# Unrolling the mixer of a decoder layer, with unnormalised k and q and the product of state and q behind the triangular solve

## Chip, cores, metric

The kernel runs on one core of a Trainium2 chip. The metric is the device time of one launch in microseconds. All arithmetic is float32; large matrix products are made from three products of rounded parts, as told below.

## What is computed

One layer (D = 1024) for a prompt of 1024 tokens and 8 short sequences of 4 tokens each (the "samples", 32 tokens, each with a cached state). Cut from the reference:

```python
h = rmsnorm(x, norm_mix)
proj = h @ w_in                       # columns: q, k, v | a, b | z | sc_b, sc_c, sc_h, all but a, b 512 wide
qkv = silu(causal_dwconv(qkv_in, w_conv_qkv))            # width 4
q = l2norm(q) * 128 ** -0.5;  k = l2norm(k)              # x / sqrt(sum x^2 + EPS), per head of 128
log_a = -exp(a_log) * softplus(proj_a + dt_bias);  beta = sigmoid(proj_b)
# gated delta rule, 4 heads, in chunks; g is the running sum of log_a in the chunk, decay = exp(g_i - g_j):
#   A = I + strict(beta * kk * decay); u, w = A^-1 applied to beta*v and beta*exp(g)*k
#   v_new = u - w S;  o = (q exp(g)) S + (q k^T decay) v_new;  S = S exp(g_last) + (k exp(g_last - g))^T v_new
o = rmsnorm(o, w_gdn_norm) * silu(z)
y_sc = sc_b * causal_dwconv(sc_c * sc_h, w_conv_sc)      # width 3
x = x + concat([o, y_sc]) @ w_out
x = x + relu(rmsnorm(x) @ w_up) ** 2 @ w_down
x = x + sigmoid(rmsnorm(x) @ w_ple_gate) * (p @ w_ple_proj)
```

## The kernel before

Each engine has a program of its own, written by hand, and the programs meet at semaphores; the order in each program is the order of execution.

**Units.** The projections run in units of 128 output columns. A unit is three thirds of 352 tokens, each 24 products on PE (TensorE): 8 blocks of k times three products of rounded parts (high by high, low part of the activations by high, high by low part of the weights), 72 products in all. For each unit SP (SyncE, whose queue issues the loads in order) loads `w_raw`, ACT (ScalarE) rounds it to `w_hi` (all its operations have the helper's line, L972), DVE (VectorE) makes `w_lo` (L1335), and each third is taken out of PSUM by DVE (for q, k and v: L1393). A unit of q, k or v is then convolved by DVE (its last three operations are L1416) and passed through a Silu by ACT. Two units are in flight: the buffers `w_raw`, `w_hi`, `w_lo`, `pre`, `cv` are doubled.

**Stages.** (1) Norm of the input: tiles of x are squared by ACT (`x_sqr`), turned, scaled and split into `act_hi`, `act_lo`; a small product makes the gates a and b. (2) Twelve units of q, k, v in that order (the products are at L555). (3) A loop of four passes. A pass has the products of four units (z, c, h, b), 288 of them at L663, dealt out by the table `STEPS` and `FILL` between the steps of two chunks of 128 tokens, so that PE has products while other engines work on the chunks. (4) The sample tokens' delta rule (L763 to L860), with the first unit of the output projection in its gaps. (5) The rest of the output projection, the MLP, and the input embedding.

**A chunk in a pass.** Three products with a matrix of ones (L682, L683, L685) sum the squares of q and k over a head's 128 rows and spread g along a row; DVE and ACT normalise k and q with them (`kn`, L1530 on DVE); PE makes k k^T and q k^T (L689, L690). DVE makes the decay matrix and from it `PT` (L1534) and `AT` (L1536). The inverse of the triangular matrix is built in six doublings, the levels (`X` and its transpose `XT`; POOL, that is GpSimd, starts them at L1935 and L1937 and masks each level's factor at L1918; PE has the products y at L703 and z at L712 and L715; DVE copies y and adds z at L1549). Then the state steps: two transposes (L724, L725), k by the state S (L726), the solve (L732), q by S and the score by v_new in one group (L741, L742), the update of S (L745), a ones sum for the output's norm (L749). The PE program of a pass, shortened:

```python
with pe.Fori(0, NSC) as j:
    fill("begin0")
    for x in range(2):
        ...
        mm(bk[0][:, :], ones[:, :], Tb[0][:, :, :], start=True, stop=True)          # L682
        ...
        fill(f"prep_norm{x}")
        pe.wait_ge(sm.qk_made, 2 * c1)
        per_head(lambda h, s: mm(bk[0][:, s], kn[x][:, h, :], kn[x][:, h, :], start=True, stop=True))
    for l in range(1, LEVELS):
        for x in range(2):
            pe.wait_ge(sm.lt_made, n1)
            per_head(lambda h, s: mm(bk[x][:, s], Tb[2 + x][:, h, :], X[x][:, h, :], ...)).then_inc(sm.y_mm, 1)
            fill(f"y{x}_{l}")
```

z goes from `cv` to DRAM (`z_spill`) and comes back chunk by chunk.

## Time and profile before

| | us |
|---|---|
| median of 3 runs | 1646.56 (1646.44 to 1648.52) |
| the profiled execution, its own time | 1649.36 |
| its span (first to last instruction) | 1647.8 |
| PE busy in it | 1568.8 (95%) |
| DVE, ACT, POOL busy | 726.5, 484.8, 299.2 |
| PE's granted clock over the span | 9 tenths or more in all but a few of 40 slices; 5 and 7 tenths in slices 15 and 16 |

The time before the first instruction and after the last is the 1.6 us between 1649.36 and 1647.8. In the trace a stretch begins and ends at instructions: the second unit's last third leaves PSUM at 62.70 us, the passes run to 572.3 us, the sample tokens and the first output unit to 652.9 us, where the second output unit starts; what comes behind it (994.9 us) the change doesn't touch. Durations of pipelined products overlap, so the distance between products, not the duration of one, is what a product takes.

### The profile page before, as it was taken

The page shows a single profiled execution, that of the slowest core. Times are in us where ns is not written, and L with a number is a line of the kernel's source. Part 1 is how long each engine was busy: PE and PEld are TensorE (multiplying, and loading weights), DVE is VectorE, ACT ScalarE, POOL GpSimd, SP SyncE. Part 2 cuts the span into 40 slices and gives each one's busy share as a digit, 9 for nine tenths or more (in the row PEclk, how much of TensorE's full clock was granted, in tenths as well). Part 3 has the DMA queues.
Part 4 walks back from the last instruction along what each step waited for, and adds up shares of the span by engine and source line. Part 5 has one row for each costly group of instructions (what it writes and reads, how often), then busy time and mean ns, then how long its engine had stood idle before and what let it go on. Part 6 is the DMA issues. An engine that isn't in the chain of part 4 may idle for free.

```text
span 1647.8 us, 26980 instructions
## 1 busy us (share of the span) xinstructions
PE 1568.8 (95%) x9857; PEld 1518.2 (92%) x9857; DVE 726.5 (44%) x1201; ACT 484.8 (29%) x818; POOL 299.2 (18%) x361
## 2 busy tenths in 40 slices
PE   7899899999999858999999999999999999999997
PEld 6899889899999846998999999999999999998997
DVE  5566555454555534225333333333333433335435
ACT  6223322223232241226321303122121313126435
POOL 5100062534526233221000000000000000032213
PEclk9999999999999957999999999999999999999998
DMA  6111110201013033321111111111111111111102
GB/s 165 38 49 40 37 39 14 64 13 52 13 39 105 0 109 93 95 76 39 52 39 51 39 51 49 42 52 39 52 44 47 47 43 52 39 51 55 49 26 106
DMA packets 135718, 86.65 MB, mean 53 GB/s; under 512 B 16507, under 2 KB 130843, under 8 KB 135654
## 3 DMA queue, kind: packets, MB, share of 16 engines
q1 hardware_dynamic: 134502, 81.48, 17.3%
q0 software_dynamic: 1152, 4.33, 0.7%
q8 instruction: 39, 0.64, 0.2%
q14 instruction: 25, 0.20, 0.0%
HBM read 74.58 MB, written 11.21 MB: 52 GB/s over the span
## 4 chain that ended last, share of the span: by engine, by line
PE 85%; DVE 6%; ACT 3%; issue 3%; POOL 1%; DMA 1%; SPq 1%; DVEq 0%; ACTq 0%; POOLq 0%
PE pg L555 64%; PE pg L663 8%; PE bk L703 3%; PE bk L712 2%; DVE act_lo L1656 1%; PE bk L870 1%; PE bk L715 1%; ACT act_hi L972 1%; DVE cv L1416 1%; ACT w_hi L972 1%; POOL XT L1937 1%; DVE qkv L1610 1%; PE bk L682 1%; PE bk L683 0%; DVE w_lo L1335 0%
## 5 line engine op out<-in xcount | busy, mean ns | idle before, releaser
L555 PE MATMUL pg<-act_hi,w_hi 128*128 128x352 f32 x1464 | 480.9, 328 | 17.9 <-issue 4.9
L555 PE MATMUL pg<-act_lo,w_hi 128*128 128x352 f32 x1464 | 473.8, 324 | 0.0
L555 PE MATMUL pg<-act_hi,w_lo 128*128 128x352 f32 x1440 | 464.3, 322 | 0.0
L555 PEld LDWEIGHTS pg<-act_hi,w_hi 128*128 128x128 f32 x1464 | 278.8, 190 | 22.4 <-issue 6.5
L555 PEld LDWEIGHTS pg<-act_lo,w_hi 128*128 128x128 f32 x1464 | 279.1, 191 | 0.0
L555 PEld LDWEIGHTS pg<-act_hi,w_lo 128*128 128x128 f32 x1440 | 272.5, 189 | 0.0
L555 PE MATMUL pg<-u_hi,w_hi 128*128 128x352 f32 x768 | 249.3, 325 | 0.0
L555 PE MATMUL pg<-u_hi,w_lo 128*128 128x352 f32 x768 | 248.9, 324 | 0.0
L555 PE MATMUL pg<-u_lo,w_hi 128*128 128x352 f32 x768 | 247.8, 323 | 0.0
L1991 POOL TENSOR_TENSOR ssq<-ssq,sq 128x352 f32<-128x352 f32 x72 | 77.8, 1094 | 890.2 <-ACT sq L972 889.3
L972 ACT ACTIVATE w_hi<-w_raw 128x1024 fp32r<-128x1024 f32 x111 | 116.7, 1051 | 323.7 <-PE pg L555 301.5
L1703 DVE TENSOR_TENSOR xres<-xres,pg 128x352 f32 (+1 forms) x192 | 99.2, 520 | 200.9 <-PE pg L555 200.9
L1335 DVE TENSOR_TENSOR w_lo<-w_raw,w_hi 128x1024 fp32r<-128x1024 f32 x110 | 141.9, 1290 | 81.3 <-ACT w_hi L972 81.3
L555 PEld LDWEIGHTS pg<-u_hi,w_hi 128*128 128x128 f32 x768 | 145.0, 189 | 0.0
L555 PEld LDWEIGHTS pg<-u_lo,w_hi 128*128 128x128 f32 x768 | 144.5, 188 | 0.0
L555 PEld LDWEIGHTS pg<-u_hi,w_lo 128*128 128x128 f32 x768 | 143.9, 187 | 0.0
L663 PE MATMUL pg<-act_hi,w_lo 128*128 128x352 f32 x384 | 131.0, 341 | 0.0
L663 PE MATMUL pg<-act_lo,w_hi 128*128 128x352 f32 x384 | 130.3, 339 | 0.0
L663 PE MATMUL pg<-act_hi,w_hi 128*128 128x352 f32 x384 | 129.3, 337 | 0.0
L972 ACT ACTIVATE sq<-tm 128x352 f32<-128x352 f32 x96 | 47.8, 498 | 231.5 <-DVE tm L1689 231.5
L1693 DVE TENSOR_TENSOR u_lo<-sq,u_hi 128x352 f32 x96 | 50.4, 525 | 129.6 <-ACT u_hi L972 129.6
L972 ACT ACTIVATE Tb<-bk 128x512 f32<-128x512 f32 (+2 forms) x76 | 44.2, 583 | 182.0 <-PE bk L703 111.8
(295 smaller groups left out, 1845.8 us busy)
## 6 DMA issues: line engine op xcount, KB each, us to landing
w_raw<-in_w_up SPq DMA_DIRECT2D x32, 512.0 KB, 4.0
w_raw<-in_w_down SPq DMA_DIRECT2D x32, 512.0 KB, 3.4
w_raw<-in_w_in SPq DMA_DIRECT2D x29, 512.0 KB, 3.9
x_tok<-in_x_prompt SPq DMA_DIRECT2D x8, 512.0 KB, 7.8
w_raw<-in_w_out SPq DMA_DIRECT2D x8, 512.0 KB, 4.9
x_col<-in_x_prompt SPq DMA_DIRECT2D x8, 512.0 KB, 3.7
w_raw<-in_w_ple_gate SPq DMA_DIRECT2D x8, 512.0 KB, 4.0
out<-y_tok SPq DMA_DIRECT2D x8, 512.0 KB, 2.9
```

The lines of the kernel that those rows point to most:

```text
L555: last = mm(pg[bank][:, 0:TH], w, a, start=i == 0, stop=i == len(terms) - 1)
L663: last = mm(pg[n][:, 0:TH], w, (act_hi, act_lo, act_hi)[r][:, k, cols(n)], start=k == 0 and r == 0, stop=k == KD - 1 and r == 2)
L682: mm(bk[0][:, :], ones[:, :], Tb[0][:, :, :], start=True, stop=True)
L703: per_head(lambda h, s: mm(bk[x][:, s], Tb[2 + x][:, h, :], X[x][:, h, :], start=True, stop=True)).then_inc(sm.y_mm, 1)
L712: last = per_head(lambda h, s: mm(zb[:, s], XT[x][:, h, :], Tb[x][:, h, :], start=True, stop=True))
L715: last = per_head(lambda h, s: mm(ztb[:, s], Tb[x][:, h, :], XT[x][:, h, :], start=True, stop=True))
L870: last = turn(bk[n][:, c:c + e - a], x_col[x][a:e, t, :], ident[a:e, a:e])
L972: return nc.scalar.activation(out, in_, func, **kw)
L1335: tt(w_lo[b % 2][:, :, :], w_raw[b % 2][:, :, :], w_hi[b % 2][:, :, :].bitcast(f32), SUB) \
L1693: tt(rows(u_lo[c % 2][:, k, cols(n)]), sq[g % 2][:, :], rows(u_hi[c % 2][:, k, cols(n)]).bitcast(f32), SUB).then_inc(sm.u_lo_made, 1)
L1703: tt(x_t, x_t, pg[g % 3][:, 0:TH], ADD).then_inc(sm.evacuated, 2)
L1991: tt(ssq[:, cols(n)], ssq[:, cols(n)], sq[g % 2][:, :], ADD).then_inc(sm.ssq_added, 1)
```

## The change

The mixer's loops are unrolled, and a table built in Python (`PLAN`) says which steps stand between which products, across chunks and units:

- Order of units: q and k first (8 units), then the four of v, then the four of z, then c, h, b in turn (12).
- The 288 products of the v units are dealt out around the inverse of chunks 0 and 1; those of the z units around the whole of the samples' delta rule (before: behind the passes); then three slots of 236 products with the inverse of the next two chunks and the state steps of the two before; the last slot has 108 products and the state steps of chunks 6 and 7. The first output unit follows (48 products of the last b unit stand in the piece called mix).
- k and q stay unnormalised. The sum of k's squares is taken by DVE from the diagonal of k k^T (`ssk`, a by-product of an operation it makes anyway), its reciprocal goes into beta; q's norm goes into the output's norm (`comb`). The two ones sums for them are gone. The rows of g come from DRAM: SP writes `g_dram` once and loads each chunk's rows, spread over all partitions (`LY`, `E`), so the third ones sum is gone too.
- The product of state and q stands right behind the triangular solve, in a PSUM bank of its own, and the score's product is added later.
- v of a chunk is turned by PE (`vturn`) ahead of its state steps; z goes through the Silu before it is spilled.
- At the start: ACT's squares of x tiles 4 to 8 stand behind the splits of `act_hi`, and the first 24 products of the first unit stand ahead of the last product of the gates; the gates' chain of logs and exponentials is spread over units 1 to 4.

The diff, cut to its core:

```diff
-STEPS = (["begin0", "prep_norm0", "prep_kk0", "prep_norm1", "prep_kk1", "prep_x0", "prep_x1"]
-         + [f"{w}{x}_{l}" for l in range(1, LEVELS) for w, x in (("y", 0), ("y", 1), ("z", 0), ("z", 1))]
-         + [f"{s}{x}" for x in range(2) for s in ("s_in", "s_solve", "s_out", "s_norm")])
-BODY_MM = 4 * KD * 9
-FILL = {"begin0": 50, "prep_norm0": 38, "prep_norm1": 38, "prep_kk0": 16, "prep_kk1": 21, "prep_x0": 4, "prep_x1": 2,
-        "s_in0": 13, "s_in1": 22, "s_solve0": 8, "s_solve1": 8, "s_out0": 8, "s_out1": 8, "s_norm0": 2}
-for _s in STEPS:
...
+def inverse_steps(s):
+    c = (2 * s, 2 * s + 1)
+    steps = [("prep", c[0], 0), ("prep", c[1], 0), ("turned", c[0], 0), ("turned", c[1], 0)]
+    for l in range(1, LEVELS):
+        steps += [("y", c[0], l), ("y", c[1], l), ("z", c[0], l), ("z", c[1], l)]
+    return steps
+def state_steps(s):
+    steps = []
+    for c in (2 * s, 2 * s + 1):
+        steps += [(k, c, 0) for k in ("into", "kturn", "solve", "update", "sum", "norm", "scale")]
+    return steps
...
+    slot([(("begin", 0, 0), 64)] + [(st, {"prep": 14, "turned": 2}.get(st[0], 8)) for st in inverse_steps(0)],
+         9 * KD * NSC)
+    smp = [("s_norm", 16), ("s_conv", 4), ("s_kk", 20), ("s_conv", 4), ("s_xt", 14), ("s_conv", 4), ("s_y", 12),
+           ("s_z", 12), ("s_state", 12), ("s_turn", 10), ("s_solve", 12), ("s_out", 20), ("s_onorm", 14)]
...
+    slot([(("s_wait", 0, 0), 6 * KD), (("s_begin", 0, 0), 4)] + steps, 9 * KD * NSC)
+    for s in range(1, NPAIR):
+        steps = [(("vturn", 2 * s - 2, 0), 6), (("vturn", 2 * s - 1, 0), 6)]
+        inv, rec = inverse_steps(s), state_steps(s - 1)
+        steps += [(rec.pop(0), 4), (rec.pop(0), 6)]
+        for i, st in enumerate(inv):
+            steps.append((st, {"prep": 14, "turned": 2}.get(st[0], 6)))
+            if i % 2 == 1 and rec:
+                steps.append((rec.pop(0), 3))
+        assert not rec
+        slot(steps, SLOT_FILL)
+    steps = [(("vturn", NTT - 2, 0), 2), (("vturn", NTT - 1, 0), 2)]
+    steps += [(st, {"scale": 0}.get(st[0], 8)) for st in state_steps(NPAIR - 1)]
+    last = 9 * KD * 3 * NSC - (NPAIR - 1) * SLOT_FILL
+    slot(steps + [(("tail", 0, 0), 0)], last - 6 * KD)
+    order.extend([(("mix", 0, 0), 3 * KD), (("mix", 1, 0), 3 * KD), (("mix", 2, 0), 0)])
+    out, at = [], 0
+    for (k, c, l), n in order:
+        out.append((k, c, l, at, at + n))
+        at += n
...
+                if k == "begin":
+                    sp.wait_ge(sm.rows_step, 2)
+                    sp.dma_start(g_dram[:, :], LY[1][0:NTT * H, 0, :]).then_inc(sm.rows_out, 16)
+                    sp.wait_ge(sm.rows_out, 16)
+                    load_rows(0)
+                    load_rows(1)
+                    load_in(U_V + 1)
+                    load_in(U_V + 2)
...
+                elif k == "vturn" and c == 0:
+                    for h in range(H):
+                        sp.wait_ge(sm.s_out_made, 2 * (h + 1))
+                        sp.dma_start(os_s[0, :, h, :, :].rearrange("b d e -> d b e"), S_in[:, h, :, :]) \
+                            .then_inc(sm.sample_states_out, 16)
+                    for x in range(2):
+                        sp.wait_ge(z_spilled[x], 16 * (NSC // 2))
+                    sp.dma_start(qkv[:, H:2 * H, TP:T], z_dram[:, :, TP:T].rearrange("h p t -> p h t")) \
+                        .then_inc(sm.zs_loaded, 16)
+                    sp.wait_ge(sm.q_o, 1)
+                    load_rows(2)
+                    load_rows(3)
+                    sp.wait_ge(sm.sample_states_out, 16 * H)
+                    sp.dma_start(E[:, :, :], g_dram[None, 0:H, :].to_broadcast([P, H, P])).then_inc(sm.ge_in, 16)
+                elif k == "solve" and c < NTT - 1:
...
-                fill("begin0")
-                for x in range(2):
-                    c1 = 2 * j + x + 1
-                    pe.wait_ge(sm.squared, 2 * c1)
-                    if x == 0:
-                        pe.wait_ge(sm.o_made, 2 * j + 1)
-                    else:
-                        pe.wait_ge(sm.at_made, 2 * j + 1)
-                    mm(bk[0][:, :], ones[:, :], Tb[0][:, :, :], start=True, stop=True)
-                    mm(bk[1][:, :], ones[:, :], Tb[1][:, :, :], start=True, stop=True)
-                    pe.wait_ge(sm.diag_made, c1)
-                    mm(bk[2][:, :], ones[:, :], X[x][:, :, :], start=True, stop=True) \
-                        .then_inc(sm.norms_summed, 1)
-                    fill(f"prep_norm{x}")
-                    pe.wait_ge(sm.qk_made, 2 * c1)
-                    per_head(lambda h, s: mm(bk[0][:, s], kn[x][:, h, :], kn[x][:, h, :], start=True, stop=True))
...
+                        pe.wait_ge(sm.x_updated, upd(c - 2, LEVELS - 1))
+                    per_head(lambda h, v: mm(A[x][:, v], qkv[:, H + h, chunk(c)], qkv[:, H + h, chunk(c)],
+                                             start=True, stop=True)).then_inc(sm.kk_mm, 1)
+                    if c > 0:
+                        pe.wait_ge(sm.pt_made, c)
+                    if c > 1:
+                        pe.wait_ge(sm.x_updated, upd(c // 2 * 2 - 1, SQUARE))
+                    per_head(lambda h, v: mm(A[2][:, v], qkv[:, H + h, chunk(c)], qkv[:, h, chunk(c)],
+                                             start=True, stop=True)).then_inc(sm.kq_mm, 1)
...
+                elif k == "solve":
+                    pe.wait_ge(sm.r_vec, 4 * (c + 1))
+                    pe.wait_ge(sm.x_updated, upd(c, LEVELS - 1))
+                    per_head(lambda h, v: mm(R[1][:, v], XT[s][x][:, h, :], rv[:, h, :], start=True, stop=True)) \
+                        .then_inc(sm.solve_mm, 1)
+                    pe.wait_ge(sm.qg_made, c + 1)
+                    pe.wait_ge(sm.ktok_made, 4 * (c + 1))
+                    per_head(lambda h, v: mm(R[0][:, v], S[:, h, :], qkv[:, h, chunk(c)], start=h == 0, stop=False)) \
+                        .then_inc(sm.os_mm, 1)
+                elif k == "update":
+                    pe.wait_ge(sm.w_made, c + 1)
+                    per_head(lambda h, v: mm(R[1][:, v], ktok[:, h, :], wn[:, h, :], start=True, stop=True)) \
+                        .then_inc(sm.upd_mm, 1)
+                elif k == "sum":
+                    per_head(lambda h, v: mm(R[0][:, v], wn[:, h, :], PT[s][x][:, h, :], start=False, stop=h == H - 1)) \
+                        .then_inc(sm.op_mm, 1)
+                elif k == "norm":
+                    pe.wait_ge(sm.comb_made, c + 1)
+                    pe.wait_ge(sm.osq_made, c + 1)
...
+            def before_sum(c):
+                if c == 0:
+                    act.wait_ge(sm.sample_states_out, 16 * H)
+                else:
+                    act.wait_ge(sm.onorm_mm, c)
+                op(comb[:, :, :], qkv[:, 0:H, chunk(c)], ACT.Square, scale=float(P) * EPS ** 0.5) \
+                    .then_inc(sm.qsq_made, 1)
+                act.wait_ge(sm.ge_in, 16 * (c + 1))
+                op(E[:, :, :], E[:, :, :], ACT.Exp).then_inc(sm.e_made, 1)
...
+                    if name == "v" and n == 1 and i > 0:
+                        silu_unit(b - 1)
+                        log_exp()
+                    if name == "z" and i == 0 and n == 1:
+                        silu_unit(b - 1)
+                    if name == "z" and n == 2:
+                        act.wait_ge(sm.evacuated, 12 * b + 12)
+                        op(cv[i % 2][:, 0:T], cv[i % 2][:, 0:T], ACT.Silu).then_inc(sm.z_silu, 1)
+                        log_exp()
...
+                if name == "v":
+                    qkv_third(b, n)
+                    if n == 2:
+                        unit_done(b, 0)
+                        convolve(b)
+                    return
...
+                if k == "prep":
+                    dve.wait_ge(gb_in[x], 16 * (c // 2 + 1))
+                    dve.wait_ge(sm.causal_made, 1)
+                    if c >= 2:
+                        dve.wait_ge(sm.lt_made, lev(c - 2, LEVELS - 1))
+                    for h in range(H):
+                        stt(AT[x][:, h, :], LY[x][:, h, :], g_tok[:, c, h:h + 1], m_inc[:, :], SUB, MIN) \
+                            .then_inc(sm.diff_made, 1)
+                    dve.wait_ge(sm.kk_mm, c + 1)
+                    if c >= 2:
+                        dve.wait_ge(sm.y_mm, lev(c - 2, LEVELS - 1))
+                    for h in range(H):
+                        stt(X[x][:, h, :], A[x][:, h * P:(h + 1) * P], 1.0, ident[:, :], MUL, MUL,
+                            accum_out=ssk[:, c, h:h + 1]).then_inc(sm.diag_made, 1)
+                    dve.wait_ge(sm.diag_made, 4 * (c + 1))
+                    ts_(sbk[:, c, :], ssk[:, c, :], EPS, None, ADD).then_inc(sm.k_step, 1)
+                    dve.wait_ge(sm.k_step, 3 * c + 1)
+                    nc.vector.reciprocal(sbk[:, c, :], sbk[:, c, :]).then_inc(sm.k_step, 1)
+                    dve.wait_ge(sm.k_step, 3 * c + 2)
+                    tt(sbk[:, c, :], sbk[:, c, :], beta[:, c, :], MUL).then_inc(sm.k_step, 1)
+                    dve.wait_ge(sm.kq_mm, c + 1)
+                    dve.wait_ge(sm.decay_made, c + 1)
+                    if c >= 4:
+                        dve.wait_ge(sm.op_mm, c - 3)
+                    tt(PT[s][x][:, :, :], heads(A[2]), AT[x][:, :, :], MUL).then_inc(sm.pt_made, 1)
```

On DVE, in the loop of before: behind the normalising of a chunk's k (L1530), with one third of a fill unit taken out (L1481) and one weight split:

```order
L1530 TENSOR_TENSOR kn<-qkv,Tb 128x512
L1343 REGISTER_ALU
L1481 TENSOR_TENSOR cv<-pg,r_b 128x352 [waits mm_done]
L1329 ISA
L1335 TENSOR_TENSOR w_lo<-w_raw,w_hi 128x1024 [waits w_hi_made]
L1534 TENSOR_TENSOR PT<-bk,Tb 128x512 [waits masked,kk_made]
```

The same engine after the change, in the first slot (v units), from the preparation of chunk 0 (`PT00`, `AT0`) to that of chunk 1 (`AT1`, `X1`):

```order
L1762 TENSOR_TENSOR PT00<-bk2,AT0 128x512 [waits decay_made,kq_mm]
L1766 SCALAR_TENSOR_TENSOR AT0<-bk0,sbk,AT0 128x128 [waits pt_made,k_step]
L1766 SCALAR_TENSOR_TENSOR AT0<-bk0,sbk,AT0 128x128 x3
L1590 TENSOR_TENSOR pre0<-pg2,r_b 128x320 [waits mm_done]
L1592 TENSOR_TENSOR pre0<-pg2,r_b 128x8x4
L1533 TENSOR_TENSOR w_lo1<-w_raw1,w_hi1 128x1024 [waits w_hi_made]
L1609 TENSOR_SCALAR cv0<-pre0,cq_w 128x1080 [waits silu_made,evacuated]
L1612 SCALAR_TENSOR_TENSOR cv0<-pre0,cq_w,cv0 128x1080 [waits conv_step] x3
L1744 SCALAR_TENSOR_TENSOR AT1<-LY1,g_tok,m_inc 128x128 [waits causal_made,gb_in1]
L1744 SCALAR_TENSOR_TENSOR AT1<-LY1,g_tok,m_inc 128x128 x3
L1750 SCALAR_TENSOR_TENSOR X1,ssk<-bk1,ident 128x128 [waits kk_mm]
L1750 SCALAR_TENSOR_TENSOR X1,ssk<-bk1,ident 128x128 x3
```

In the loop of before no convolution stood between the parts of a pass; now the whole of one (L1609, L1612) stands between the preparation of chunk 0 and that of chunk 1.

On SP's queue before, at the head of the passes, the weights' loads follow each other:

```order
L442 UNCONDITIONAL_BRANCH
L442 ISA
L414 ISA [waits w_lo_made]
L414 DMA w_raw<-in_w_in 128x8x128
```

After the change, at the head of the first slot (first fence) and of the third, the first with state steps (second fence), with the writes of the samples' states (`out<-S_in`), the samples' z (`qkv<-z_spill`) and the rows of g (`LY`, `E`) in the same queue:

```order
L585 DMA g_rows<-LY 32x128 [waits rows_step]
L566 DMA LY<-g_rows 128x512 [waits rows_out]
L566 DMA LY<-g_rows 128x512
L524 DMA w_raw<-in_w_in 128x8x128 [waits w_lo_made] x4
```

```order
L612 DMA qkv<-z_spill 128x4x32 [waits z_spilled1,z_spilled0]
L566 DMA LY<-g_rows 128x512 [waits q_o]
L566 DMA LY<-g_rows 128x512
L618 DMA E<-g_rows 128x512 [waits sample_states_out]
L628 DMA qkv<-z_spill 128x4x128 [waits kt_mm]
L621 DMA E<-g_rows 128x512 [waits qg_made]
L524 DMA w_raw<-in_w_in 128x8x128 [waits w_lo_made]
```

Loads of weights now stand behind transfers that wait for other engines: the first behind the way of g's rows to DRAM and back, the later ones behind the spilled z and the states.

## Rows read from the trace of the kernel before

**Rows 1.** The page: busy time of the engines.
```profile
PE 1568.8 (95%) x9857; PEld 1518.2 (92%) x9857; DVE 726.5 (44%) x1201; ACT 484.8 (29%) x818; POOL 299.2 (18%) x361
```

**Rows 2.** Busy time in stretches; the first line names the columns.
```profile
core 0: us, PE busy (x) PEld busy (x) DVE busy (x) ACT busy (x) POOL busy (x), PEclk, DMA share, GB/s
0.00:62.70 62.70, 50.61 (x297) 47.35 (x298) 31.41 (x48) 30.02 (x53) 23.76 (x80) 0.95 0.52 124
62.70:213.00 150.30, 140.96 (x854) 136.75 (x853) 95.19 (x142) 48.92 (x64) 17.48 (x39) 0.97 0.16 43
308.90:404.50 95.60, 92.97 (x642) 88.02 (x641) 48.24 (x90) 26.19 (x42) 39.86 (x39) 0.98 0.11 33
572.30:652.90 80.60, 51.92 (x248) 41.37 (x248) 35.89 (x48) 24.28 (x40) 27.73 (x21) 0.65 0.33 93
```

**Rows 3.** The waits of PE: total us, times, longest.
```profile
PE bk L703 <- POOL Tb L1918: 7.4, 4, 1.9
...
PE pg L555 <- DVE pre L1393: 4.4, 1, 4.4
```

**Rows 4.** The chain that ended last: start, length, what.
```profile
24.66 1.14 ACT x_sqr L972 x2
...
40.75 0.86 PE bk L626 x2
...
803.69 689.64 PE pg L555 x4296
```

**Rows 5.** PE in order of time, full clock: a level's products, transposes.
```profile
425.14 1.05 PE L703 MATMUL bk<-X,Tb 128*128 128x128 f32 x8
...
426.36 1.05 PE L703 MATMUL bk<-X,Tb 128*128 128x128 f32 x8
...
464.31 0.60 PE L725 MATMUL bk<-ident,X 128*128 128x128 f32 x4
464.74 1.06 PE L726 MATMUL bk<-S,kn 128*128 128x128 f32 x8
```

**Rows 6.** PE in order of time, 17 products behind a wait of 8.2 us.
```profile
616.22 0.49 PE L555 MATMUL pg<-act_lo,w_hi 128*128 128x352 f32 x1
616.51 0.49 PE L555 MATMUL pg<-act_hi,w_lo 128*128 128x352 f32 x1
...
620.62 0.42 PE L555 MATMUL pg<-act_lo,w_hi 128*128 128x352 f32 x1
```

**Rows 7.** DVE in order of time, the end of one unit.
```profile
62.70 0.49 DVE L1393 TENSOR_TENSOR pre<-pg,r_b 128x320 f32<-128x320 f32 x1 [3.22 <-PE pg L555]
...
63.80 1.22 DVE L1335 TENSOR_TENSOR w_lo<-w_raw,w_hi 128x1024 fp32r<-128x1024 f32 x1 [0.50 <-ACT w_hi L972]
...
65.75 4.10 DVE L1416 SCALAR_TENSOR_TENSOR cv<-pre,cq_w,cv 128x1080 f32<-128x1080 f32 x3
```

**Rows 8.** DVE in order of time, operations of a chunk.
```profile
406.41 1.12 DVE L1522 TENSOR_SCALAR Tb<-bk,g_tok 128x128 f32<-128x128 f32 x4 [5.12 <-ACT Tb L972]
...
423.82 0.69 DVE L1549 TENSOR_TENSOR X<-X,bk 128x512 f32<-128x512 f32 x1 [5.35 <-PE bk L712]
```

**Rows 9.** POOL in order of time, the start of one inverse.
```profile
413.80 1.29 POOL L1935 TENSOR_TENSOR XT<-AT,m_lev 128x512 f32<-128x512 f32 x1 [1.12 <-DVE AT L1536]
415.17 2.14 POOL L1937 TENSOR_TENSOR XT<-ident,XT 128x512 f32<-128x512 f32 x1
417.27 2.48 POOL L1918 TENSOR_TENSOR Tb<-AT,m_lev 128x512 f32<-128x512 f32 x2
```

**Rows 10.** ACT in order of time: a table load, the next operation.
```profile
604.67 1.28 ACT L1146 ACT_TABLE_LOAD   x1
605.97 1.06 ACT L972 ACTIVATE act_hi<-qkv 128x1024 fp32r<-128x1024 f32 x1
```

**Rows 11.** DMA issues: KB each, median us to landing.
```profile
w_raw<-in_w_in SPq DMA_DIRECT2D x29, 512.0 KB, 3.9
...
z_spill<-cv POOLq DMA_DIRECT2D x4, 528.0 KB, 4.0
```

1759 lines of the change are left out of this document (940 added, 819 removed).

## The prediction

> **What bounds the kernel now.** The table of busy times comes first: PE has products during 95% of the span, no other engine more than 44% [rows 1]. So the time is PE's work plus its waits, and the change can win only by taking work off PE, or by filling the stretches in which it stands. The busy times in stretches show where these are [rows 2]. In a pass (308.90 to 404.50, 95.60 us) PE is busy for 92.97 at a clock of 0.98, with next to no slack. In the samples' stretch (572.30 to 652.90, 80.60 us) it is busy for 51.92, and at a clock of 0.65. Up to 62.70 it is busy for 50.61. The list of PE's waits [rows 3] names what a pass still waits for, POOL's masked factor (7.4 us in 4 waits), and one wait of 4.4 us at the evacuation of a q unit. In the chain of waits the products of the MLP follow at 689.64 / 4296 = 0.1605 us each [rows 4], the price of a product below.
>
> **Prices of PE's work.** Two level products in order of time stand 426.36 - 425.14 = 1.22 us apart [rows 5]; two fill products (0.32) are between, so a group of four heads costs 0.90. The transposes of four heads cost 464.74 - 464.31 = 0.43 [rows 5]. A sum with the matrix of ones over 512 columns is one product in the code and two records in the trace; the chain gives 0.86 for the two [rows 4], nearly a group's 0.90, which has as many columns, so a sum costs 0.86 and not half of it.
>
> **The work removed.** Before, a chunk has 20 groups of four heads (k k^T, q k^T, six y, seven z, k S, solve, two in the output, update), two sets of transposes and four ones sums: 20 x 0.90 + 2 x 0.43 + 4 x 0.86 = 22.3 us. A pass is then 288 x 0.1605 + 2 x 22.3 = 90.8, against 95.6 measured: 4.8 lost. After, the groups and transposes are as many, and one ones sum is left: 19.7. Eight chunks save 8 x 3 x 0.86 = 20.6 us. A reciprocal and an accumulated sum on DVE replace them: its four diagonal operations are like L1522, 1.12 us [rows 8], and lie under 14 products (2.2 us) in a steady slot.
>
> **The front.** The squares of five x tiles (1.14 us for two pieces in the chain, [rows 4]) leave ACT's path ahead of the splits: 5 x 1.14 = 5.7 us, and 24 products of the first unit (3.9) go into the wait for the last split. Sum 9.7; low bound 3.8, if the tiles' loads are what is late next. So what is at 62.70 comes at 53.0.
>
> **The account from 62.7 to 652.9.** It is 590.2 us. Products: 27 units x 72 x 0.1605 = 312.0. Chunks: 8 x 22.3 = 178.6. The samples' own PE work and the turns of x: the stretch's 51.92 less 72 products (11.6) is 40.3 at the slow clock and, times 0.65, 51.92 gives 33.7, less 11.6 is 22.1. I take 32, between them. Sum 522.6, so 67.6 us are lost today to waits and the slow clock, about 35 of them in the samples' stretch, 4 x 4.8 = 19 in the passes. After, the work is 312.0 + 157.6 + 32, and 1 for the turn of g into rows, 502.6, and 53.0 + 502.6 = 555.6. With L for the losses after, the second output unit starts at 555.6 + L, against 652.9. **The whole question is L: at 97.3 the gain is gone.**
>
> **What L is made of.** The samples move behind 288 products, so their chain of small steps (a wait of 8.2 us among them today) has cover: slot 1 has 288 x 0.1605 = 46 us of it for some 13 steps, and only what waits longer than the 12 to 20 products between steps is lost. Against this stand new waits, and each of them is made by one engine's bulk work standing ahead of a chain step:
>
> - Slot 0, 27 us. (a) SP sends g's rows to DRAM and back before the next weights. A load of weights lands in 3.9 us, a spill in 4.0 [rows 11]; the way there and back ahead of them makes the weights of unit 10 some 7 us late, and with them `w_hi`, `w_lo` (1.22, [rows 7]), and the last k unit's convolution: PE waits 5 to 7. (b) In the order of DVE the convolution (from a third's evacuation at 62.70 to its last operations' end at 65.75 + 4.10 = 69.85 is 7.15 us, [rows 7]) stands between the preparations of chunks 0 and 1, and POOL's start of the inverse (1.29 + 2.14, then 2.48 for two masks, [rows 9]) behind that: the first y of chunk 1 waits about 7. (c) Two more convolutions stand ahead of the step that puts a z product into X (0.69, [rows 8]): 7.15 + 0.7 less a cover of 4.2 to 4.4 is 3.7, twice. Each such wait is followed by products at about half clock (1.2 GHz, not 2.4): in the stretch behind the wait of 8.2 us they stand 616.51 - 616.22 = 0.29 apart up to 620.62 [rows 6], 15 to 17 of them, so 17 x 0.13 = 2 us more. Sum 6 + 2 + 7 + 2 + 2 x (3.7 + 1.3) = 27.
> - Slot 1, 7 us: the samples' squares wait for the last v unit (its last third, 24 products or 3.9 us, and 7.15 to the end of the convolution are 11.05 with the Silu behind it; 52 products ahead of the samples' sums cover 8.3), then Silus of z with table loads (1.28 each, [rows 10]).
> - Slot 2, 14 us: `E` and the rows of chunks 2 and 3 stand in SP's queue behind the last z unit's spill: evacuation 0.5, `w_hi` 1.05, table 1.28 [rows 10], Silu 1, spill 4.0 [rows 11] make 7.8, two loads of rows at 2 to 4 each put `E` at about 12.9. PE is through its covered steps in about 6 and waits in pieces of 2 to 3.
> - Slots 3 and 4: today's 4.8 for a pass, 5 each. Last slot: 8 products (1.3 us) cover each step of a chain whose steps take 1.5 to 2.5: 8.
>
> L = 27 + 7 + 14 + 10 + 8 = 66. Then 555.6 + 66 = 621.6, 31.3 earlier than 652.9; what follows is untouched. 1649.4 - 31.3 = 1618.1 for the profiled execution, whose own time is 2.8 above the median of the runs shown, so **1615.3**.
>
> **A rule against it.** ACT changes its table more often: 18 loads between the v units and the end of slot 1. In the trace a load takes 1.28 us and the next operation starts 0.02 us behind its end (604.67 + 1.28 = 605.95, start 605.97) [rows 10], so 23 us of ACT's time in 92 us, beside some 30 of other work: hidden, but for the places above. The Trainium skill (ScalarE: Activation LUTs, "What ACT_TABLE_LOAD costs") puts a drain of the pipeline on top of the load, about twice the load alone; the row shows none of it behind a load. By the page it would be about 1.38 us more for each, 25 us over all if every one lay on PE's path, and the time about 1640.
>
> **The rivals.**
>
> A. The forecast, L from 50 to 80: 1600 to 1630.
>
> B. The new waits are covered: the row loads take under 2 us and the squares wait for nothing. Then L is about today's share of the passes (19) and half of slot 0, some 35: 1616 - 31 = 1584. For it: before, a pass loses only 4.8 with the same chain. Against: DVE's order really has whole convolutions between steps.
>
> C. The loads of rows are late at every slot, not at slots 0 and 2 alone, or the samples' chain is longer than its 46 us: 20 more, 1630 to 1643. For it: the samples' stretch takes 80.6 us today, less 11.6 of products, for 46 us of cover, though it also holds 28 us of waits and runs at 0.65. The table loads at the page's price would end here too.
>
> D, on the other side: slower. DVE's and ACT's bulk work isn't covered in any slot. There are 20 unit ends from slot 0 on; the split of weights and evacuation (2.3 us each) in front of a chain step would give 46, four convolutions before and in slot 0 with their Silus and the z Silus 34, and 20 waits with slow products behind each 2.3 x 20 = 46: L = 126, which is 29 over 97.3, so 1675.6. It decides from L = 97.3, an average wait of about 1.2 us at each of the roughly 80 steps. Against it: steps have 6 to 14 products, 1 to 2.2 us, besides the other chunk's group. A pass today has the same kind of bulk work at L = 4.8.
>
> E. The change gives nothing: L within 94 and 101 (0.2%, 3.3 us, is about what a measurement of this kernel tells from no change).
>
> **How the numbers follow.** A 0.50, B 0.25, C 0.17, D 0.05, E 0.03. Faster is A + B + C = 0.92, same 0.03, slower 0.05. The range leaves out about 1 in 10 below (B's lower half) and 1 in 10 above: 1585 to 1641. The unknowns reach as far: the front at 3.8 adds 6; the parts of L at slot 0 and slot 2, the largest, are each good to some 10; the samples' work at 22 or 40 moves little, since it stands on both sides.
>
> **What the profile after would show.** The end of the first unit near 41.5 us and of the second near 53; if the second stays above 57, the loads bound the front. One ones sum for a chunk in place of four, and no others. PE's waits in slot 0 for ACT's Silu (about 5), at a y product for DVE's `X` (about 7) and twice at a y or z for DVE's step on X (3.7); in slot 1 one for ACT before the samples' ones sums; at the start of slot 2 for `E` or `comb`. The second output unit at about 621 in place of 652.9, and behind it 995 us as now. The prediction is wrong if L is spread evenly over the slots (C or D), or if the clock stays low behind short waits, so that a wait costs more than its 2 us, or if the first slot's waits are missing (B). In slots 3 and 4 a distance above 85 us (236 products and two chunks are 77.3) would speak for D.

## The result and the profile after

The changed kernel takes 1623.52 us (median of 4 runs, 1622.55 to 1624.63) against 1646.82 (4 runs, 1646.44 to 1648.52): ratio 0.9857, 95% interval 0.9840 to 0.9874, 23.3 us faster. The forecast was 1615.3 with a range of 1585 to 1641: the right side and case (A), 8.2 us too low. The profiled execution took 1623.29 us, its span 1621.5.

The page after, first the busy times (before: [rows 1]):

```profile
PE 1548.1 (95%) x9812; PEld 1508.4 (93%) x9812; DVE 730.2 (45%) x1261; ACT 489.4 (30%) x872; POOL 291.6 (18%) x346
```

PE's share is the same 95%, with 20.7 us less of busy time. The stretches, which answer to [rows 2]: first the rest of the k and q units, then the slot of the v units, the slot of the z units and the samples, and the first slot with state steps:

```profile
core 0: us, PE busy (x) PEld busy (x) DVE busy (x) ACT busy (x) POOL busy (x), PEclk, DMA share, GB/s
60.60:130.30 69.70, 69.70 (x443) 69.58 (x442) 48.04 (x71) 16.89 (x27) 3.49 (x19) 1.00 0.13 33
130.30:236.20 105.90, 81.87 (x530) 80.55 (x529) 59.32 (x101) 27.41 (x38) 25.89 (x27) 0.87 0.21 54
236.20:316.80 80.60, 77.92 (x449) 67.19 (x448) 31.21 (x54) 25.96 (x35) 13.58 (x18) 0.92 0.25 75
316.80:407.00 90.20, 81.43 (x578) 79.04 (x577) 48.19 (x103) 29.16 (x55) 39.62 (x38) 0.96 0.18 52
```

PE stands for 24.0 us in the v slot and hardly at all in the samples' slot (2.7 us; before, 28.7 in their stretch). The waits of PE, over the whole execution (compare [rows 3]):

```profile
PE bk L852 <- DVE XT L1778: 11.6, 2, 6.3
PE bk L852 <- DVE X L1770: 9.5, 2, 8.6
PE bk L902 <- DVE wn L1791: 8.4, 3, 3.7
...
PE bk L910 <- POOL comb L2180: 3.7, 3, 2.1
PE bk L838 <- ACT qkv L1136: 3.6, 1, 3.6
...
PE bk L885 <- POOL S L2189: 2.2, 1, 2.2
```

Before, the chain of waits had the MLP's 4296 products start at 803.69 [rows 4]; after:

```profile
777.09 689.62 PE pg L688 x4296
```

They start 26.6 us earlier and take as long as before. The table follows the prediction's landmarks: its value, and where the changed kernel's trace has it. L is a stretch's length less its work, priced as in the prediction.

| landmark or loss | forecast | measured |
|---|---|---|
| second unit's last third leaves PSUM | 53.0 | 60.55 |
| v slot: L | 27 | 105.9 - 73.2 = 32.7 |
| slot 2: L | 14 | 90.2 - 77.3 = 12.9 |
| slots 3, 4: L | 10 | (81.0 - 77.3) + (82.9 - 77.3) = 9.3 |
| last slot: L | 8 | 41.3 - 25.0 - 12.5 = 3.8 |
| z slot and first output unit: L, the rest | 7 | 7.0 |
| second output unit starts | 621.6 | 628.9 |

The sum of L is 628.9 - 60.6 - 502.6 = 65.7, forecast 66. The miss of the total is in the first line; the lines for L miss in both directions and cancel.

### The profile page after: what moved, and what is told of

The parts are those of the page before. It is cut to its first block, busy times and chain, and to the rows that moved or that the text cites. A ratio compares the mean times of both kernels' runs of the same rounds, so it can differ in the third digit from the quotient of the medians.

```text
span 1621.5 us, 25803 instructions
## 1 busy us (share of the span) xinstructions
PE 1548.1 (95%) x9812; PEld 1508.4 (93%) x9812; DVE 730.2 (45%) x1261; ACT 489.4 (30%) x872; POOL 291.6 (18%) x346
## 3 DMA queue, kind: packets, MB, share of 16 engines
q1 hardware_dynamic: 139254, 85.15, 18.3%
## 4 chain that ended last, share of the span: by engine, by line
PE 84%; DVE 7%; ACT 2%; issue 2%; POOL 2%; DMA 0%; SPq 0%; DVEq 0%; POOLq 0%; ACTq 0%
PE pg L688 62%; PE pg L806 10%; PE bk L852 3%; PE bk L866 2%; DVE cv L1612 1%; DVE act_lo L1881 1%; PE bk L870 1%; PE bk L1013 1%; DVE AT L1744 1%; POOL act_lo L2186 1%; PE bk L824 1%; PE bk L1117 1%; PE bk L993 1%; ACT w_hi L1136 0%; PE bk L902 0%
## 5 line engine op out<-in xcount | busy, mean ns | idle before, releaser
L688 PE MATMUL pg<-act_hi,w_hi 128*128 128x352 f32 x1344 | 438.6, 326 | 10.4 <-issue 4.6
L688 PE MATMUL pg<-act_lo,w_hi 128*128 128x352 f32 x1344 | 432.6, 322 | 0.0
L688 PE MATMUL pg<-act_hi,w_lo 128*128 128x352 f32 x1320 | 423.8, 321 | 0.0
L688 PEld LDWEIGHTS pg<-act_hi,w_hi 128*128 128x128 f32 x1344 | 253.4, 189 | 14.4 <-issue 8.5
L688 PEld LDWEIGHTS pg<-act_lo,w_hi 128*128 128x128 f32 x1344 | 254.0, 189 | 0.0
L688 PEld LDWEIGHTS pg<-act_hi,w_lo 128*128 128x128 f32 x1320 | 248.0, 188 | 0.0
L806 PE MATMUL pg<-act_hi,w_hi 128*128 128x352 f32 x480 | 164.9, 344 | 0.0
L806 PE MATMUL pg<-act_hi,w_lo 128*128 128x352 f32 x480 | 164.6, 343 | 0.0
L806 PE MATMUL pg<-act_lo,w_hi 128*128 128x352 f32 x480 | 164.4, 342 | 0.0
L806 PEld LDWEIGHTS pg<-act_lo,w_hi 128*128 128x128 f32 x480 | 94.1, 196 | 3.6 <-issue 3.4
```

What stands on the lines that cost most here:

```text
L688: last = mm(pg[bank][:, 0:TH], w, a, start=i == 0, stop=i == len(terms) - 1)
L806: last = mm(pg[n][:, 0:TH], w, (act_hi, act_lo, act_hi)[r][:, k, cols(n)], start=k == 0 and r == 0, stop=k == KD - 1 and r == 2)
```

## Experiments

All are the changed kernel with one edit, or a few where said, timed beside the kernel before. Its medians beside them were 1647.92, 1648.46 and 1646.56 us, so a difference of 1 to 2 us between two kernels' medians says little, and the intervals of the first five edits below overlap the base's. Their effects are read from "landmarks", the times of the same instructions in two profiled executions. These scatter too: in eight executions with the same start the first ones sums begin at 41.84 to 43.07 us, the v slot takes 105.6 to 107.7 us where no edit touches it, and the z slot takes 80.6 us in some executions and 76.8 in others (see the last section).

**The changed kernel again**, as a base. 

> The changed kernel itself, unaltered, as the base for the kernels that are run beside it. Its median should lie within 1.5 us of 1623.5; every difference below is taken against this one.

Measured: 1624.04 (1622.42 to 1626.72), ratio 0.9861 (0.9842 to 0.9881). The ones sums at the start begin at 42.56 us, the turns of x ahead of the second output unit at 628.43.

**The squares back in their loop.**

```diff
-                if t < 4:
-                    square(t)
+                square(t)
...
-            for t in range(4, NTT + 1):
-                square(t)
```

> The changed kernel with the squares of x tiles 4 to 8 back in ACT's loop, between the splits of act_hi. By the prediction's term (five squares of 1.14 us leave ACT's path) it is 5 to 6 us slower than the changed kernel. The rival, read from the trace after: the splits waited for DVE and for PE's turns, not for ACT (ACT idles 3.8 and 1.9 us between splits), and the postponed squares now hold up the norm of x (r_tok at 38.7 us, before 33.3), on which the ones sums at 42.0 wait. By the rival it is the same within 1.5 us, or faster.

Measured: 1622.54 (1619.26 to 1626.60), ratio 0.9856 (0.9836 to 0.9876). The ones sums start at 41.12, 1.4 us earlier than the base and 0.7 earlier than the earliest of the eight executions. Two later kernels with the same start have them at 41.30 and 42.67, so whether anything is gained isn't clear; the prediction's 5.7 us slower isn't there for this edit alone.

**The first group back.**

```diff
-            first_group(0)
             pe.wait_ge(sm.xlo_even, NTT + 1)
             pe.wait_ge(sm.xlo_odd, NTT + 1)
             ab_group(2)
+            first_group(0)
             first_group(1)
```

> The changed kernel with the first 24 products of the first unit back behind the last product of the gates a and b. By the prediction's term they filled a wait of 3.5 us, so it is 3 to 4 us slower. The rival: PE's start of the ones sums at 42.0 us is set by ACT's postponed squares, and PE only waits in another place; then within 1 us of the changed kernel.

Measured: 1626.05 (1624.12 to 1627.42), ratio 0.9869 (0.9851 to 0.9887). The ones sums start at 44.59, 2.0 us later than the base and 1.5 later than the latest of the eight executions, about half of the term of 3.9. It lies between the two expectations.

**Both edits of the start undone.** 

> The changed kernel with both of its edits to the start undone: ACT's squares in their loop, and the first 24 products behind the gates' last. If the two are independent: the group costs 2.0, the squares give 1.4 back, so the ones sums start 0.6 us later than in the changed kernel, at 42.6 to 43.2 us. By the prediction's account 9.7 us later. The rival: with the group back PE's order is what bounds and the squares are hidden either way, about 44.5.

Measured: 1628.25 (1626.04 to 1628.91), ratio 0.9883 (0.9863 to 0.9903). The ones sums start at 47.95, 5.4 us later than the base. All three expectations fall: the two edits stand in for each other. With the group early, PE works while ACT squares; with the squares late, the split is ready early. Either covers most: PE waits for the last split of the activations 1.6 us with the group alone back, not at all with the squares alone back, and 3.6 us with both back, and it then goes on at half clock. The second unit's last third leaves PSUM at 66.18, so with both edits undone the start is 3.5 us slower than that of the kernel before (62.70).

**The ones sums back.**

```diff
+                    for _ in range(3):
+                        mm(A[x][:, :], ones[:, :], qkv[:, H:2 * H, chunk(c)], start=True, stop=True)
                     per_head(lambda h, v: mm(A[x][:, v], qkv[:, H + h, chunk(c)], qkv[:, H + h, chunk(c)],
```

> The changed kernel with three sums with the matrix of ones over 512 columns added to each chunk's preparation (24 in all, results overwritten, nothing else altered), which prices the ones sums that the change removed. By the account (PE is what bounds, 0.86 us each) 24 x 0.86 = 20.6 us slower. The rival: a part of them would lie in PE's waits (the preparations of chunks 0 to 3 are followed by waits), then 13 to 17 us.

Measured: 1626.95 (1624.30 to 1627.81), ratio 0.9872 (0.9853 to 0.9891): 2.9 us, below both expectations. Each set of three does take 2.6 us where it stands (412.60 to 415.18 in its trace). By landmarks the v slot grows by 5.7 us (of which up to 2 can be scatter), slot 2 shrinks by 1.4, slots 3 and 4 grow by 3.9 and 1.4: 9.6 of 20.6. The wait for v_new shrinks from 8.4 us in three to 1.7 in two, since DVE is done while PE sums. The z slot is 3.9 us shorter in this execution, and that isn't the sums' doing (see the clock, below).

**The product of state and q one step later.**

```diff
                     per_head(lambda h, v: mm(R[1][:, v], XT[s][x][:, h, :], rv[:, h, :], start=True, stop=True)) \
                         .then_inc(sm.solve_mm, 1)
-                    pe.wait_ge(sm.qg_made, c + 1)
-                    pe.wait_ge(sm.ktok_made, 4 * (c + 1))
-                    per_head(lambda h, v: mm(R[0][:, v], S[:, h, :], qkv[:, h, chunk(c)], start=h == 0, stop=False)) \
-                        .then_inc(sm.os_mm, 1)
                 elif k == "update":
                     pe.wait_ge(sm.w_made, c + 1)
+                    pe.wait_ge(sm.ktok_made, 4 * (c + 1))
                     per_head(lambda h, v: mm(R[1][:, v], ktok[:, h, :], wn[:, h, :], start=True, stop=True)) \
                         .then_inc(sm.upd_mm, 1)
+                    pe.wait_ge(sm.qg_made, c + 1)
+                    per_head(lambda h, v: mm(R[0][:, v], S[:, h, :], qkv[:, h, chunk(c)], start=h == 0, stop=False)) \
+                        .then_inc(sm.os_mm, 1)
```

> The changed kernel with the product of state and q moved from behind the triangular solve to behind the product that updates the state, one step later. Theory: those 0.9 us of work stand in the time in which DVE makes v_new from the solve; where PE waits for it anyway (3.7, 1.8 and 2.9 us, chunks 0, 2 and 4), the wait grows by 0.9 each, and in the other five chunks the products between cover it: 2 to 4 us slower. Rival: DVE's update of the state becomes late as well and the next chunk's k by state waits for it, 6 us or more; or everything is covered, within 1 us.

Measured: 1626.24 (1625.87 to 1627.10), ratio 0.9875 (0.9856 to 0.9894): 2.2 us. The three waits for v_new grow from 8.4 to 11.2 us, 0.9 each, in its trace:

```profile
PE bk L899 <- DVE wn L1791: 11.2, 3, 4.6
```

By landmarks slot 2 grows by 1.9 us and slot 4 by 2.3, though slot 4 varies by 1.5 without this edit. So the placement that gives the change its name is worth some 2 us, no more than the runs can tell apart.

**The samples without cover.**

```diff
-        steps.append(((k, count[k], 0), n))
-    steps += [(("s_put", i, 0), 8) for i in range(2 * H)]
-    slot([(("s_wait", 0, 0), 6 * KD), (("s_begin", 0, 0), 4)] + steps, 9 * KD * NSC)
+        steps.append(((k, count[k], 0), 0))
+    steps += [(("s_put", i, 0), 0) for i in range(2 * H)]
+    slot([(("s_wait", 0, 0), 9 * KD * NSC - 4), (("s_begin", 0, 0), 4)] + steps, 9 * KD * NSC)
```

> The changed kernel with all 284 products of the z units ahead of the samples' delta rule and none between its steps, which takes its cover away in the same place of the program. Theory (the prediction's account): PE stood for some 29 us in the samples' stretch before, with about half the clock for a part of it, and has next to no waits in it now, so 25 to 35 us slower. Rival: the small products and their low clock were the cost, not the waits: under 15 us.

Measured: 1638.33 (1635.36 to 1641.76), ratio 0.9947 (0.9929 to 0.9964): 14.3 us. The samples' steps take 52 us by themselves, PE busy for 39.5 of them at a clock of 0.57:

```profile
283.00:335.00 52.00, 39.52 (x163) 26.95 (x162) 19.40 (x34) 9.96 (x19) 13.55 (x14) 0.57 0.14 44
```

From the g sum to slot 2 it loses 17.7 us (228.1 against 210.4), and slot 2 gives 6.5 back, since the last z is long spilled when it starts. The size forecast, 25 to 35, was too high, and the rival's range (under 15) holds. As a cause the runs show both: the z slot grows from 80.6 to 97.5 us, PE stands for 12.5 of it in place of 2.7, some 10 us more, and the other 7 go with the lower clock (0.77 over the slot, 0.92 in the base). A third of the 28.7 us of waits before stood for things that are ready by now in any order (the states' load, 5.0 us; the first sums, 4.3).

**The weights first on SP's queue.**

```diff
                 if k == "begin":
+                    load_in(U_V + 1)
                     sp.wait_ge(sm.rows_step, 2)
...
                     load_rows(1)
-                    load_in(U_V + 1)
```

> The changed kernel with the load of the first v unit's successor (unit 10) issued on SP's queue ahead of the way of g's rows to DRAM and back. Theory: those weights land 6 us late (w_hi at 135.6 us, last evacuation before it at 130.3), and DVE's split and the last k unit's convolution with them; then PE's wait of 3.6 us before the first preparation goes, with some 2 us of half clock behind it: 5 to 6 us faster from the g sum to the samples' first product. Rival: DVE's convolution and ACT's Silu of that unit are late by themselves, and at most 1 us is gained.

Measured: 1618.40 (1617.62 to 1619.94), ratio 0.9820 (0.9801 to 0.9838): 5.6 us. By landmarks only 3.2 of it is in the v slot: the wait of 3.6 us is gone, but the first y product waits 9.9 in place of 8.6, since the convolution ahead of it is where it was. In its profiled execution the z slot is 3.7 us shorter and slot 2 0.9 longer, which isn't the edit's doing; so the median may flatter it.

**The convolution dealt out**: in the first three v units each of its four operations on DVE stands behind a step of the inverse. POOL's saving of those units' last columns moves one third later with it.

```diff
+                if U_V <= b < U_V + 3:
+                    taps.extend((tap, w) for w in range(CW))
+                else:
+                    for w in range(CW):
+                        tap(w)
...
+                if taps and k in ("y", "z", "turned") and not (k == "turned" and c == 0):
+                    f, w = taps.pop(0)
+                    f(w)
                 for b, n in thirds(a, e):
                     third(b, n)
```

> The changed kernel with the four operations of each of the first three v units' convolutions dealt out on DVE, one behind each step of the inverse, in place of all four at the unit's end. Theory: the whole convolution ahead of a chain step is what PE waits for in the first slot (8.6, 6.3 and 5.3 us, each with about 2 us of half clock behind), so 15 to 24 us faster, with the convolutions themselves as long as now. Rival: POOL's start of the inverse and ACT's table loads are late next and keep most of the waits: under 8 us faster.

Measured: 1605.71 (1602.93 to 1606.91), ratio 0.9742 (0.9722 to 0.9761): 18.3 us, by landmarks 19.4 in the v slot. The waits of PE from the g sum to the samples, first the base, then this kernel:

```profile
PE bk L852 <- DVE XT L1778: 11.6, 2, 6.3
PE bk L852 <- DVE X L1770: 8.6, 1, 8.6
PE bk L838 <- ACT qkv L1136: 3.6, 1, 3.6
```

```profile
PE bk L852 <- DVE X L1781: 5.3, 1, 5.3
PE bk L838 <- ACT qkv L1136: 3.6, 1, 3.6
PE bk L852 <- DVE XT L1789: 1.0, 2, 0.5
```

The same DVE work, in another order. What is left of the wait of 8.6 us, 5.3, is DVE's preparation of chunk 1 (150.91 to 157.41 us in this trace). It stands ahead of DVE's transpose of chunk 0's `XT` into `X`, which the first y product of chunk 0 reads: POOL has had `XT` ready since 152.15, DVE transposes it at 157.33. No run here moved that transpose ahead of the preparation.

**The rows first on SP's queue, the zeroed state ahead of the spill.** In SP's program the wait for the spilled z and its load move behind the loads of `LY` and `E`; on POOL:

```diff
+                        if i == NSC - 1:
+                            pool.wait_ge(sm.sample_states_out, 16 * H)
+                            nc.gpsimd.memset(S[:, :, :], 0.0).then_inc(sm.s_zeroed, 1)
                         pool.wait_ge(sm.z_silu, i + 1)
```

> The changed kernel with the rows of g for chunks 2 and 3 and of E on SP's queue ahead of the wait for the spilled z, and POOL's zeroing of the state ahead of the last z spill. Theory: the start of the third slot waits for these (2.2 us for the zeroed state, 3.7 us for the solve's copy behind late rows, 0.8 for the score), so 5 to 8 us faster in that slot. Rival: the Silu of z with its table loads on ACT holds the copies of v in the same place, and at most 2 us are gained.

Measured: 1619.35 (1615.11 to 1620.59), ratio 0.9817 (0.9796 to 0.9837): 4.7 us, by landmarks 3.7 in slot 2. The wait for the zeroed state (2.2) and that for the score (0.7) are gone; the wait for v_new stays at 3.4, so late rows weren't its cause. What the traces show of its cause is in the last section.

**All of these together** (weights first, convolution dealt out, rows first, squares back). 

> The changed kernel with the three edits above together (weights first, convolution dealt out, rows first) and ACT's squares back in their loop. If the waits are apart from each other the gains add up: 5.5 + 19 + 6 + 1.5 = 32 us faster, about 1592. Rival: as with the ones sums, what is taken out at one place comes back as a wait at the next; then half of it or less, above 1607.

Measured: 1594.15 (1591.65 to 1596.22), ratio 0.9674 (0.9654 to 0.9694): 29.9 us under the changed kernel, 54 under the one before. By themselves the four edits gave 5.6, 18.3, 4.7 and 1.5, together 30.1: the gains add up, though two of them lie in the same slot, where they take away different waits. By landmarks the v slot is 22.6 us shorter than the base's and slot 2 3.6; the z slot is 3.4 us shorter in this execution too, which no edit explains.

**The small products dealt out**, in the joined kernel, between the z units' products.

```diff
                 for i in range(NB):
                     c = (h * NB + i) * 8
                     last = mm(bk[4][:, c:c + 8], S_in[:, h, i, :], F0[:, c:c + 8], start=True, stop=True)
+                    fill(a + (e - a) * i // NB, a + (e - a) * (i + 1) // NB)
```

> The joined kernel with the 64 small products of the samples' q, k by the cached states (128 x 8) dealt out one by one between the z units' products, in place of runs of 16 and 32. In three of the profiled executions the granted clock is 0.5 for some 8 us at these runs, in the others it isn't, and the slot is 3.7 us longer where it is. Theory: the runs of small products lower the clock; dealt out they don't, and the slot takes 67.8 us or less in every execution, the median 0 to 3 us below the joined kernel's. Rival: the clock falls anyway, or each change between small and large products costs time: the same or slower.

Measured: 1592.88 (1589.75 to 1592.91), ratio 0.9666 (0.9649 to 0.9683), 1.3 us under the joined kernel, with ranges that overlap. Its z slot takes 76.9 us, the joined kernel's 77.2, and the clock in 242 to 258 us is 0.79 in both. So it tells little: the joined kernel's profiled execution had no long stretch at half clock either, and what dealing out does about one isn't shown. It has the lowest median here. (The 64 small products of the expectation, in runs of 16 and 32, are records of the trace; the program has 32 products, in runs of 8, 8 and 16.)

## Why the prediction was right, and where it missed

**The account and the price of products held** where a row can show it: the k and q units' stretch has 432 products, 69.3 us at 0.1605, and takes 69.70 without a gap; three ones sums take 2.6 us, 0.86 each.

**The v slot's three mechanisms were there.** (a) SP issues g's rows at 127.28 and 128.69 and the weights behind them at 129.55; ACT splits them at 135.61, 5.3 us behind the unit's last evacuation, DVE at 136.70:

```profile
127.28 0.33 SPq L585 DMA_DIRECT2D g_rows<-LY  x1
128.69 0.82 SPq L566 DMA_DIRECT2D LY<-g_rows  x2
129.55 22.13 SPq L524 DMA_DIRECT2D w_raw<-in_w_in  x4
```

```profile
135.61 1.06 ACT L1136 ACTIVATE w_hi<-w_raw 128x1024 fp32r<-128x1024 f32 x1 [8.36 <-issue]
```

The forecast wait was 5 to 7, measured 3.6. (b) On POOL the start of chunk 0's inverse, on DVE the whole convolution, then chunk 1's preparation, and only then the transpose into chunk 0's `X`:

```profile
150.08 2.34 POOL L2170 TENSOR_TENSOR XT<-ident,XT 128x512 f32<-128x512 f32 x1
151.20 1.80 DVE L1609 TENSOR_SCALAR cv<-pre,cq_w 128x1080 f32<-128x1080 f32 x1
153.04 5.01 DVE L1612 SCALAR_TENSOR_TENSOR cv<-pre,cq_w,cv 128x1080 f32<-128x1080 f32 x3
157.97 1.13 DVE L1744 SCALAR_TENSOR_TENSOR AT<-LY,g_tok,m_inc 128x128 f32<-128x128 f32 x4
161.28 1.13 DVE L1766 SCALAR_TENSOR_TENSOR AT<-bk,sbk,AT 128x128 f32<-128x128 f32 x4
162.33 0.70 DVE L1770 STREAM_TRANSPOSE X<-XT 128x512 f32<-128x512 f32 x1
```

and PE's first y product, which is chunk 0's:

```profile
163.17 2.05 PE L852 MATMUL bk<-X,LY 128*128 128x128 f32 x8 [8.62 <-DVE X L1770]
```

Forecast 7, measured 8.6, but not by the path that was forecast. The prediction had chunk 1's first y wait, for POOL's start of chunk 1's inverse behind DVE. It is chunk 0's first y that waits, though its `XT` was ready at 152.42: in DVE's order the step `turned` of chunk 0 (L1770) stands behind the whole preparation of chunk 1, and this behind the convolution. Chunk 1's first y, at 167.37, waits for nothing more. The two later waits, forecast at 3.7 each, measured 6.3 and 5.3: the transpose of the inverse (L1778) stands behind the same convolution and the step on X too, and DVE's operations last longer beside POOL's (the split of the weights 2.21 us ahead of both, against 1.22 [rows 7]; the convolution above 1.80 and 5.01, against 0.78 and 4.10). With 24 us of waits and the half clock behind them L was 32.7 for 27. The dealt-out convolution shows that the convolution's place is the larger part of the cause.

**The step that failed is "the front": 9.7 us, measured 2.1.** Two things were wrong with it. The term added the squares and the group, each at its full size; the runs show that they overlap: undone alone they move the ones sums by -1.4 and 2.0 us, undone together by 5.4. And it took the rest of the start as unchanged, which it isn't: DVE makes the gates' `w_hi` behind a low part, 1.0 us later than before (16.98, before 16.01), and needs 1.30 us for it in place of 0.22, while POOL works from 16.93 to 18.19 (see the last section). PE waits 2.6 us for it (before, 0.4) and soon runs at half clock:

```profile
16.98 1.30 DVE L1530 TENSOR_TENSOR w_hi<-w_raw,w_hi 128x64 fp32r<-128x64 f32 x1
```

```profile
18.43 0.40 PE L688 MATMUL pg<-act_hi,w_hi 128*128 128x352 f32 x1 [2.60 <-DVE w_hi L1530]
...
20.93 0.49 PE L688 MATMUL pg<-act_hi,w_hi 128*128 128x352 f32 x1
...
22.61 0.60 PE L746 MATMUL bk<-ident,x_tok 128*128 128x128 f32 x4
```

Before, PE was back at the turns of x at 19.15: 3.5 us are lost here. No run put that order back, so this part rests on the traces; it fits the run with both edits undone, whose start is 3.5 us slower than the one before. The prediction had said that a second unit above 57 would mean that the loads bound the front. It was at 60.55, but PE's waits for the loads of x are 6.6 us, before 6.7, so the loads aren't what was added.

**Slot 2** was forecast at 14 and took 12.9, but only in part for the reason given. The zeroed state stands behind the spill, as `E` does, and moving both ahead gave 3.7 us (the run with rows first); the 3.7 us for v_new have another cause.

**That L came out at 65.7 for 66 is in part luck.** The v slot was 5.7 us over its forecast, the last slot 4.2 under, slot 2 and slots 3 and 4 together 1.8 under. The z slot's 7.0 are right in number only: the forecast wait of the samples' first sums for ACT (11.05 less a cover of 8.3) is 0.8 us in the trace, and 3.7 of the 7.0 are a low clock that other executions of the same program part don't have.

**The 20.6 us for the ones sums were the size of the work, not of the gain.** Put back, they cost 2.9 us in the median and 9.6 by landmarks: a part of what was taken out had come back as waits, of which the one for v_new is seen (8.4 us with the sums out, 1.7 with them in); the rest isn't traced. The prediction's sum came out all the same, as L was estimated for the kernel after, with such waits in it.

**The samples** are covered as forecast (2.7 us of standing in their slot); bare in the same place they cost 14.3 us more.

**The prediction's rule against it, on table loads,** would have given about 1640. There are 16 such loads from the v slot to the end of the z slot (forecast 18). The trace agrees with the rows of before and not with the rule:

```profile
143.99 1.28 ACT L1204 ACT_TABLE_LOAD   x1
145.28 0.63 ACT L1136 ACTIVATE AT<-AT 128x512 f32<-128x512 f32 x1
```

The next operation starts 0.01 us behind the load's end. Rival D fell: L is 65.7, not above 97. The section on the change said that no convolution stood between the parts of a pass before. One does, the shorter one of the c, h and b units (L1492, L1495: 367.47 to 371.21 us), between the state steps of two chunks, and PE, with fill products there, doesn't wait for it; so bulk work alone in DVE's order doesn't make a wait.

Of the 26.6 us by which the MLP's products start earlier, 2.6 lie behind the last landmark: the output projection starts at a granted clock of 0.90 before (652.90 to 680.00), behind a stretch in which PE stands for 28.7 us, and of 1.00 after (628.90 to 656.00), where it doesn't follow such a stretch. That the prediction had not.

## What to carry to other kernels

Where one engine interleaves bulk work with the steps of a dependent chain, look at what stands ahead of each chain step in its queue: cutting the convolutions of three units (5 to 7 us each) into four pieces between steps was worth 18 us here, while putting 20 us of work back on the bounding engine cost only 3 to 10. The step that waits can be another chunk's than the one that the bulk work precedes, so follow the queue down to the operation that the waiting engine reads. Price removed work as an upper bound: it is a gain only where the engine isn't about to wait. Don't add the gains of two edits that fill the same wait. And look at a length in several executions before an edit is given the credit.

## What the runs showed of the hardware

**DVE's operations last longer while POOL works.** In slot 2 four operations of DVE that take 1.13 us elsewhere (157.97, above) take 4.08, while POOL runs three operations from 333.74 to 337.68. One by one:

```profile
334.01 1.18 DVE L1744 SCALAR_TENSOR_TENSOR AT<-LY,g_tok,m_inc 128x128 f32<-128x128 f32 x1
335.12 1.44 DVE L1744 SCALAR_TENSOR_TENSOR AT<-LY,g_tok,m_inc 128x128 f32<-128x128 f32 x1
336.48 1.35 DVE L1744 SCALAR_TENSOR_TENSOR AT<-LY,g_tok,m_inc 128x128 f32<-128x128 f32 x1
337.75 0.34 DVE L1744 SCALAR_TENSOR_TENSOR AT<-LY,g_tok,m_inc 128x128 f32<-128x128 f32 x1
```

```profile
333.74 1.30 POOL L2168 TENSOR_TENSOR XT<-AT,m_lev 128x512 f32<-128x512 f32 x1 [2.21 <-DVE AT L1766]
335.12 1.28 POOL L2170 TENSOR_TENSOR XT<-ident,XT 128x512 f32<-128x512 f32 x1
336.37 1.31 POOL L2097 TENSOR_TENSOR LY<-AT,m_lev 128x512 f32<-128x512 f32 x1
```

Each of the first three ends 0.14 to 0.17 us behind one of POOL's; the fourth, alone, takes 0.34. It is the same in slots 3 and 4 (4.07 and 3.18 us for the four). DVE makes v_new at 341.75, behind these four and the rest of chunk 3's preparation, and PE waits 3.7 us for it. Without the 3 us the wait would be mostly gone, by an estimate from these rows; no run tried it. With the rows first it is the same (4.10 and 3.4). The Trainium skill (SBUF — State Buffer, "Who interferes with whom") says that DVE and GpSimd share a pair of ports as an exclusive lock, and that a DVE instruction with two inputs in SBUF contends there with a GpSimd instruction that reads SBUF. L1744 has two such inputs (`LY`, `m_inc`), and the rows agree. By it the cure would be to keep POOL's start of one chunk away from DVE's preparation of the next, which no run here tried.

**The clock falls in a run of small products without a wait.** PE's 32 products of 128 x 8 (64 records) stand in runs of 8, 8 and 16. The clock granted in one stretch of 16 us around them, first in the base, then in the kernel with the squares back:

```profile
266.00:282.00 16.00, 16.00 (x81) 15.60 (x81) 2.42 (x7) 3.35 (x3) 0.00 (x0) 0.58 0.00 0
```

```profile
264.00:280.00 16.00, 14.01 (x98) 13.35 (x98) 2.69 (x8) 5.29 (x5) 0.60 (x1) 0.89 0.21 66
```

The program there is the same, PE is never idle in the first, and the z slot takes 80.6 us in the one and 76.9 in the other. The last run of 16 takes 6.5 us in five of the profiled executions (the changed kernel's two, and those with the group back, with the convolution dealt out and with the rows first) and 3.4 to 3.7 in six others; nothing lies between. So 3.7 us of the z slot come and go between executions, and comparisons of single executions above leave them out. With one profiled execution of most kernels, what decides it stays open.
